# Expert feed-forward in steps of 512 columns, with gate and up panels apart and one running order across experts

## The reference

```
def swiglu(h, wg, wu, wd):
    return (jax.nn.silu(h @ wg) * (h @ wu)) @ wd

def moe_swiglu(h, router, wg, wu, wd):
    ...
    out = jnp.zeros(h.shape, jnp.float32)
    for e in range(N_EXPERTS):
        out = out + combine[..., e:e + 1] * swiglu(h, wg[e], wu[e], wd[e]).astype(jnp.float32)
```

## Time and profile before

| what | value |
|---|---|
| median of three runs | 1997.97 us |
| span of the profiled execution | 1991.5 us |
| PE busy | 1860.5 us (93%) |
| DVE busy | 1538.0 us (77%) |
| ACT busy | 1140.7 us (57%) |
| DMA moved | 485.36 MB, mean 244 GB/s |
| experts, first up matmul to last down matmul | 946.7 to 1972.4 us of the span |

### The profile page before, as it was taken

One profiled execution on the slowest core, in us unless ns is written; L12 is line 12 of the kernel. 1 busy time (PEld: TensorE's weight loads), 2 busy tenths in 40 slices (PEclk: granted clock), 3 DMA queues, 4 the chain that ended last, 5 costly groups with the idle time before them and its releaser, 6 DMA issues.

```text
span 1991.5 us, 29581 instructions
## 1 busy us (share of the span) xinstructions
PE 1860.5 (93%) x10776; PEld 1626.4 (82%) x10776; DVE 1538.0 (77%) x1598; ACT 1140.7 (57%) x1037; POOL 5.1 (0%) x13
## 2 busy tenths in 40 slices
PE   6999889899989999896999999999999999999997
PEld 6988788799979888785787887878878788788785
DVE  3979867544449799576788888879878888898886
ACT  4335544444343355543676776767767667676774
POOL 0000000000000000000000000000000000000000
PEclk9999999999988899897999999999999999999998
DMA  6434333755334344335899999999989999999993
GB/s 227 149 119 157 127 107 114 264 190 188 108 120 136 110 149 137 106 128 180 275 367 315 367 365 313 367 308 360 367 299 367 330 337 365 312 367 359 309 366 117
DMA packets 346936, 485.36 MB, mean 244 GB/s; under 512 B 16992, under 2 KB 270944, under 8 KB 346736
## 3 DMA queue, kind: packets, MB, share of 16 engines
q1 hardware_dynamic: 345808, 479.65, 71.5%
q0 software_dynamic: 1056, 4.70, 0.6%
HBM read 483.24 MB, written 1.05 MB: 243 GB/s over the span
## 4 chain that ended last, share of the span: by engine, by line
PE 75%; DVE 14%; ACT 5%; issue 4%; DMA 1%; SPq 0%; ACTq 0%; DVEq 0%
PE pair L750 53%; PE aux L750 16%; DVE lo_ring L1234 5%; ACT hi_ring L387 2%; PE aux L1134 2%; PE pair L1157 1%; DVE arena L1466 1%; DMA raw_ring<-in_w_in 1%; DVE arena L1415 1%; DVE arena L1401 1%; DVE x L1777 1%; DVE small L1414 1%; DVE pair L1391 0%; DVE arena L1480 0%; ACT arena L432 0%
## 5 line engine op out<-in xcount | busy, mean ns | idle before, releaser
L1234 DVE TENSOR_TENSOR lo_ring<-raw_ring,hi_ring 128x2048 fp32r<-128x2048 f32 (+2 forms) x278 | 623.6, 2247 | 140.3 <-ACT hi_ring L387 136.3
L387 ACT ACTIVATE hi_ring<-raw_ring 128x2048 fp32r<-128x2048 f32 (+2 forms) x278 | 521.1, 1878 | 191.3 <-PE pair L750 151.3
L1234 DVE TENSOR_TENSOR lo_ring<-arena,hi_ring 128x2048 fp32r<-128x2048 f32 x183 | 419.4, 2292 | 78.9 <-ACT hi_ring L387 72.3
L750 PE MATMUL pair<-lo_ring,hT_hi 128*128 128x512 f32 (+3 forms) x992 | 392.3, 395 | 19.9 <-DVE lo_ring L1234 17.5
L750 PE MATMUL pair<-hT_lo,hi_ring 128*128 128x256 f32 x1328 | 389.5, 293 | 20.1 <-ACT arena L432 7.7
L750 PE MATMUL pair<-hT_hi,lo_ring 128*128 128x256 f32 x1328 | 383.9, 289 | 0.0
L750 PE MATMUL pair<-hT_hi,hi_ring 128*128 128x256 f32 x1328 | 383.3, 289 | 0.0
L750 PE MATMUL pair<-hi_ring,hT_hi 128*128 128x512 f32 (+3 forms) x992 | 382.3, 385 | 0.0
L750 PE MATMUL pair<-hi_ring,hT_lo 128*128 128x512 f32 (+3 forms) x992 | 381.3, 384 | 0.0
L387 ACT ACTIVATE hi_ring<-arena 128x2048 fp32r<-128x2048 f32 x183 | 349.4, 1914 | 46.2 <-PE pair L750 36.2
L750 PEld LDWEIGHTS pair<-hT_lo,hi_ring 128*128 128x128 f32 x1328 | 263.1, 198 | 27.9 <-ACT arena L432 10.0
(11 more groups left out here) (277 smaller groups left out, 1984.8 us busy)
## 6 DMA issues: line engine op xcount, KB each, us to landing
arena<-in_md SPq DMA_DIRECT2D x128, 512.0 KB, 5.7
raw_ring<-in_w_in SPq DMA_DIRECT2D x120, 512.0 KB, 4.5
raw_ring<-in_mg SPq DMA_DIRECT2D x120, 512.0 KB, 5.4
raw_ring<-in_mu SPq DMA_DIRECT2D x120, 512.0 KB, 6.4
arena<-in_mg SPq DMA_DIRECT2D x104, 512.0 KB, 5.2
arena<-in_mu SPq DMA_DIRECT2D x104, 512.0 KB, 6.2
raw_ring<-in_md SPq DMA_DIRECT2D x96, 512.0 KB, 5.2
raw_ring<-in_w_br SPq DMA_DIRECT2D x32, 512.0 KB, 4.6
```

Of the source, the lines that this page charges most:

```text
L387: nc.scalar.activation(hi_ring[:, h, 0:cols], raw(slot)[:, 0:cols], ACT.Copy).then_inc(hi_ready, 1)
L750: ins = pe.matmul(out, l, r, start=first and n == 0, stop=last and n == 2, skip_group_check=True)
L1234: nc.vector.tensor_tensor(lo_ring[:, h, 0:cols], raw(slot)[:, 0:cols], hi_ring[:, h, 0:cols].bitcast(f32), ALU.subtract).then_inc(lo_ready, 1)
```

## The change

An expert now has seven steps of 512 hidden columns with six panels each: two gate panels, two up panels, and the two down panels of the step before it. Gate goes into the first bank of `pair0` and up into its second, transposes go into `pair1`; there is no alternation. The order gate, up, down of the step before runs on through the end of an expert: the two last down panels of an expert stand in the first step of the next. The gather of the next expert's tokens is moved to step 5, ahead of its down panels, `hx_hi` and `hx_lo` to the end of step 6. `turn_pick` is in step 3, the scatters in step 1, one ahead of the down panels and one behind them. Each engine has one loop per expert with all seven steps written out. Rows of gate and up weights that a DMA reads are 512 columns (2 KB) instead of 256 (1 KB). Since the last down panels no longer end inside the loop, they follow it after the branch that skips the extra blocks.

```diff
--- before.py
+++ after.py
-EXP_STEPS = F_EXP // STEP_F
+EXP_F = 512
+EXP_STEPS = F_EXP // EXP_F
...
-EXP_PANELS = 3 * EXP_STEPS
+EXP_PANELS = 6 * EXP_STEPS
...
-        hid_hi = sb("hid_hi", [128, 2, STEP_F], f32r)
-        hid_lo = sb("hid_lo", [128, 2, STEP_F], f32r)
+        hid_hi = sb("hid_hi", [128, EXP_F], f32r)
+        hid_lo = sb("hid_lo", [128, EXP_F], f32r)
...
+        def exp_at(n, k):
+            return k if isinstance(n, int) and n == 0 else 6 * n - 2 + k
+        def exp_slot(n, k):
+            return k if isinstance(n, int) and n == 0 else (4 + k) % FRING
+        def exp_use(n, k):
+            return 0 if isinstance(n, int) and n == 0 else (n - 1 if k < 2 else n)
...
+            def exp_panel(n, k, src, width):
+                slot = exp_slot(n, k)
+                p = EXP_BASE + exp_at(n, k)
+                v = raw(slot).rearrange("p (k n) -> p k n", n=width)
+                h = v.shape[1] // 2
+                sp.wait_ge(lo_ready, p - (FRING - 1))
+                sp.dma_start(v[:, 0:h, :], src[:, 0:h, :]).then_inc(raw_in[slot], 16)
+                sp.dma_start(v[:, h:2 * h, :], src[:, h:2 * h, :]).then_inc(raw_in[slot], 16)
+            def exp_up(n, e, s):
+                for w, k0 in ((mg, 0), (mu, 2)):
+                    for kh in range(2):
+                        exp_panel(n, k0 + kh, w[bass.ds(e, 1), kh * 512:(kh + 1) * 512, s * EXP_F:(s + 1) * EXP_F]
+                                  .rearrange("a (k p) n -> p (a k) n", p=128), EXP_F)
+            def exp_down(n, e, s):
+                for q in range(2):
+                    r = s * EXP_F + q * 256
+                    exp_panel(n, 4 + q, md[bass.ds(e, 1), r:r + 256, :].rearrange("a (k p) n -> p (a k) n", p=128), D)
+            def expert(j, e, before):
+                n0 = j * EXP_STEPS
+                for s in range(EXP_STEPS):
+                    exp_up(n0 + s, e, s)
+                    if s:
+                        exp_down(n0 + s, e, s - 1)
+                    elif before is not None:
+                        exp_down(n0, before, EXP_STEPS - 1)
+            expert(0, 0, None)
+            with sp.Fori(1, NE) as j:
+                expert(j, j, j - 1)
...
+            def exp_silu(n):
+                act.wait_ge(panel_used, EXP_BASE + exp_at(n, 1) + 1)
+                act.wait_ge(S["hid_done"], DENSE_STEPS + n)
+                nc.scalar.activation(ar(A_SG, EXP_F), pairs[0][:, 0:EXP_F], ACT.Silu).then_inc(S["gu_silu"], 1)
+            def exp_hid_hi(n):
+                act.wait_ge(S["hid_turned"], n + 1)
+                nc.scalar.activation(hid_hi[:, :], pairs[1][:, 0:EXP_F], ACT.Copy).then_inc(S["hid_hi_done"], 1)
...
+                for s in range(EXP_STEPS):
+                    n = j * EXP_STEPS + s
+                    if not (first and s == 0):
+                        exp_hi(n, 0)
+                        exp_hi(n, 1)
+                    exp_hi(n, 2)
+                    if not (first and s == 0):
+                        exp_hid_hi(n - 1)
+                    if s == 1 and not first:
+                        output_hi(j - 1, EXP_BASE + exp_at(j * EXP_STEPS, 5) + 1)
+                    exp_hi(n, 3)
+                    if not (first and s == 0):
+                        exp_hi(n, 4)
+                    exp_silu(n)
+                    if not (first and s == 0):
+                        exp_hi(n, 5)
+                    if s == 3:
+                        pickT_copy(j)
+                act.wait_ge(panel_used, EXP_BASE + exp_at((j + 1) * EXP_STEPS - 1, 3) + 1)
+                hx_hi(j + 1)
...
+            exp_end = (m + NE) * EXP_STEPS
+            for q in range(2):
+                to_hi(EXP_BASE + exp_at(exp_end, q), exp_slot(1, q), EXP_USE0[exp_slot(1, q)] + exp_use(exp_end, q), PANEL,
+                      (EXP_BASE + exp_at(1, q)) % HRING)
+                if q == 0:
+                    exp_hid_hi(exp_end - 1)
+            output_hi(m + (NE - 1), EXP_BASE + exp_at(exp_end, 1) + 1)
...
+            def exp_weights(n, k, width):
+                h = (EXP_BASE + (k if isinstance(n, int) and n == 0 else exp_at(1, k))) % HRING
+                pe.wait_ge(lo_ready, EXP_BASE + exp_at(n, k) + 1)
+                return weights(h, width)
+            def exp_up(n):
+                for g in range(2):
+                    for kh in range(2):
+                        w = exp_weights(n, 2 * g + kh, EXP_F)
+                        for k in range(4):
+                            a = (4 * kh + k) * 128
+                            ins = split_mm(pairs[0][:, g * EXP_F:(g + 1) * EXP_F], (hxh[:, a:a + 128], hxl[:, a:a + 128]),
+                                           (w[0][:, k, :], w[1][:, k, :]), kh == 0 and k == 0, kh == 1 and k == 3)
+                        ins.then_inc(panel_used, 1)
+            def exp_turn(n):
+                pe.wait_ge(S["hid_done"], DENSE_STEPS + n + 1)
+                for k in range(EXP_F // 128):
+                    ins = pe.transpose(pairs[1][:, k * 128:(k + 1) * 128], ar(A_HID + k * 128, 128), C("ident"))
+                ins.then_inc(S["hid_turned"], 1)
+            def exp_down(n, k0, s):
+                pe.wait_ge(S["hid_lo_done"], DENSE_STEPS + n)
+                for q in range(2):
+                    w = exp_weights(n, k0 + q, 512)
                     for half in range(2):
                         for k in range(2):
-                            ins = split_mm(aux[:, half * 512:(half + 1) * 512],
-                                           (hid_hi[:, s0 % 2, k * 128:(k + 1) * 128], hid_lo[:, s0 % 2, k * 128:(k + 1) * 128]),
+                            o = (2 * q + k) * 128
+                            ins = split_mm(aux[:, half * 512:(half + 1) * 512], (hid_hi[:, o:o + 128], hid_lo[:, o:o + 128]),
                                            (w[0][:, 2 * k + half, :], w[1][:, 2 * k + half, :]),
-                                           s0 == 0 and k == 0, s0 == EXP_STEPS - 1 and k == 1)
+                                           s == 0 and q == 0 and k == 0, s == EXP_STEPS - 1 and q == 1 and k == 1)
                     ins.then_inc(panel_used, 1)
 
+            def turn_pick(j, first):
+                if not first:
+                    pe.wait_ge(S["x_added"], 2 * j)
+                for b in range(NB):
+                    ins = pe.matmul(aux[:, 1024 + b * 128:1152 + b * 128], pick[:, b, :], ident_r[:, :], start=True, stop=True)
+                ins.then_inc(S["pick_turned"], 1)
+            def expert(j, first=False):
                 pe.wait_ge(S["hx_lo_done"], j + 1)
...
+                for s in range(EXP_STEPS):
+                    n = j * EXP_STEPS + s
+                    exp_up(n)
+                    if s == 1 and not first:
+                        scatter(j - 1, 0)
+                    if s == 3:
+                        turn_pick(j, first)
+                    if s == 5:
+                        pe.wait_ge(S["pickT_done"], j + 1)
+                        gather(j + 1)
+                    if s:
+                        exp_down(n, 4, s - 1)
+                    elif not first:
+                        exp_down(n, 4, EXP_STEPS - 1)
+                    if s == 1 and not first:
+                        scatter(j - 1, 1)
+                    exp_turn(n)
...
+            exp_down((m + NE) * EXP_STEPS, 0, EXP_STEPS - 1)
...
+            def exp_hid(n):
+                dve.wait_ge(S["gu_silu"], DENSE_STEPS + n + 1)
+                dve.wait_ge(panel_used, EXP_BASE + exp_at(n, 3) + 1)
+                if not (isinstance(n, int) and n == 0):
+                    dve.wait_ge(S["hid_turned"], n)
+                nc.vector.tensor_tensor(ar(A_HID, EXP_F), pairs[0][:, EXP_F:2 * EXP_F], ar(A_SG, EXP_F), ALU.mult)\
+                  .then_inc(S["hid_done"], 1)
+            def exp_hid_lo(n):
+                dve.wait_ge(S["hid_hi_done"], DENSE_STEPS + n + 1)
+                nc.vector.tensor_tensor(hid_lo[:, :], pairs[1][:, 0:EXP_F], hid_hi[:, :].bitcast(f32), ALU.subtract)\
+                  .then_inc(S["hid_lo_done"], 1)
...
+                for s in range(EXP_STEPS):
+                    n = j * EXP_STEPS + s
+                    opening = first and s == 0
+                    if not opening:
+                        exp_lo(n, 0)
+                        exp_lo(n, 1)
+                    exp_lo(n, 2)
+                    if not opening:
+                        exp_hid_lo(n - 1)
+                    if s == 1 and not first:
+                        output_lo(j - 1)
+                    if s == 4:
+                        dve.wait_ge(S["pickT_done"], j + 1)
+                        make_pick(j + 1)
+                    exp_lo(n, 3)
+                    if not opening:
+                        exp_lo(n, 4)
+                        exp_lo(n, 5)
+                    exp_hid(n)
+                    if s == 1 and not first:
+                        add(j - 1, 0)
+                    if s == 2 and not first:
+                        add(j - 1, 1)
```

(28 more changed lines are left out.)

108 lines of the change are left out of this document (26 added, 82 removed).

## The result

The changed kernel takes 1970.14 us, the median of six runs (1960.30 to 1971.33), beside 1996.64 for six runs of the kernel before (1988.46 to 2001.74). These medians lie 26.5 us apart; the ratio on record isn't that of the medians, it is 0.9847 with a 95% interval of 0.9826 to 0.9867, which is 30.5 us less (26.6 to 34.7). Forecast were 1966 us in a range of 1957 to 1985, and faster. Both held.

The account below looks back on a forecast made before the run. PE's matmul stream was taken to bound the experts, with the rest to be won where an expert ends. Terms summed to -32.2 us: span 1991.5 to 1959.3, plus 6.5 outside, about 1966 us, range 1957 to 1985.

Parts of the forecast that it names:

- (a): Between experts: PE's wait for the next expert's tokens goes, 2.59 us seven times, 18.1 us less.
- (b): Behind the token wait: slow clock after idle PE goes, 1.57 us at four of seven boundaries, 6.3 us less.
- (c): `turn_pick` and the turn behind it: no wait for DVE's late product, 0.81 x 7 = 5.7 us less.
- (d): First scatter and the turn behind it: scatters now lie between panels without waits, 0.32 x 7 = 2.2 us less.
- (e): Turns inside experts: one of four transposes replaces two of two, 56 steps of 512 save 3.1 us.
- three tight places: Handover, output split in step 1, second add in step 2: 0.2, 0.2, 0 us spare; cost 0, range 0 to 1 each.
- (f): First expert: the product stands ahead of the next gate panel's lo on DVE, 0.9 us lost.
- (g): End of last expert: 1.6 us wait for the last split plus 0.7 for a hi part, 2.3 us lost.
- Tight places: Rival: tokens 1 us later, other tight places 0.3 each, slow clock at four of seven boundaries; 1983 us, chance 0.14.
- DVE as the bound: Rival: longer lo parts or a late product let DVE set the step; 2033 us at 2.8 per part, chance 0.07.
- Loop code that doesn't stay: Rival: PE's longer loop body is fetched anew at six returns, up to 29.7 us; 1995.6 or about 1981, chance 0.10.
- The 6.5 us outside it: Program time beyond the profiled span: 1997.97 - 1991.5, added to the span of 1959.3 to give 1965.8 us.

Follow-up runs that it names:

- late_tokens: Changed kernel with gather, `hx_hi` and `hx_lo` put back behind the turn of an expert's last step; 1988.59 us, ratio 0.9950.
- filled kernel: Kernel before the change, with 18 matmuls of unused result ahead of PE's wait for the tokens at seven boundaries; 1990.22 us, ratio 0.9954.
- one loop: Changed kernel with the number of extra blocks read before the first expert and a single loop over all blocks; 1962.93 us, ratio 0.9823.

## Why the prediction was right, and where it was not

**(a) The wait for the tokens, 18.1.** Right. No wait of PE at the handover is left; late_tokens brought 7 x 2.5 back.

**(b) The slow clock behind it, 6.3.** Right: 6.8 in the filled kernel, and 1.00 at the handovers after. The late tokens cost 1.9 each for it instead of 0.9 per handover, as all seven fell and not four, three of them for 6.8 us and not 3.4. So this term belongs to an execution of a given kernel, not to the code alone.

**(c), (d), (e) `turn_pick`, scatter and turns, 5.7 + 2.2 + 3.1.** Right in sum. The time of one expert can be read from PE's branch at the end of the loop (line, duration min/median/max in ns, first and last start), which answers to the earlier trace rows:

```profile
L1284 PEldq COMPARE_BRANCH  x7: 83/215/217, 1185.1 to 1925.9; - x7
L1288 PEldq COMPARE_BRANCH  x1: 3591/3591/3591, 1926.9 to 1926.9; - x1
```

(1925.9 - 1185.1) / 6 = 123.47 us, forecast 123.4. Before it was 127.57 without slow clock; less 2.59 for the wait, 1.51 per expert is left for these three terms, 1.55 forecast. (The 1.51 is net of the 0.2 that is lost in step 2, see the tight places.) The two places themselves:

```profile
1099.15 0.39 PE L1272 MATMUL aux<-hT_lo,pickT 128*128 128x512 f32 x1
...
1100.06 0.60 PE L1221 MATMUL pair<-consts,arena 128*128 128x128 f32 x4
1100.42 0.47 PE L815 MATMUL pair<-lo_ring,hT_hi 128*128 128x512 f32 x1
...
1128.43 0.33 PE L1241 MATMUL aux<-ident_r,pick 128*128 128x128 f32 x2
1128.60 0.45 PE L815 MATMUL aux<-lo_ring,hid_hi 128*128 128x512 f32 x1
```

The turn follows the scatter's four matmuls after 0.91, without a wait, and `turn_pick` costs 0.17; with its turn it took 1.17 in the earlier trace rows. A turn of four costs 0.36 until the next panel starts and, from the step of 16.78 less 6 x 2.72, 0.46 in all; I had taken 0.49.

**The three tight places, taken at 0.** Right for two; the third costs 0.2 us per expert. The handover, on ACT (`hx_hi`, then two hi parts) and on DVE (product, `hx_lo`, two lo parts), start and duration:

```profile
1182.94 1.03 ACT L733 ACTIVATE hT_hi<-aux 128x1024 fp32r<-128x1024 f32 x1 [0.88 <-PE pair L815]
1183.86 3.71 ACT L432 ACTIVATE hi_ring<-arena 128x2048 fp32r<-128x2048 f32 x2
```
```profile
1184.30 0.68 DVE L1826 TENSOR_TENSOR arena<-pair,arena 128x512 f32<-128x512 f32 x1
1184.90 1.22 DVE L1813 TENSOR_TENSOR hT_lo<-aux,hT_hi 128x1024 fp32r<-128x1024 f32 x1
1186.03 4.48 DVE L1308 TENSOR_TENSOR lo_ring<-arena,hi_ring 128x2048 fp32r<-128x2048 f32 x2
```

The lo parts start at 1186.03, and 2.35 later, by the handover of the prediction, is 1188.38; PE starts at 1188.46. So 0.1 us is to spare where I had 0.2. The forecast was right by little, and it isn't shown how much more DVE may take at this place before PE waits.

In step 1, with the split of the finished output, no gap of PE shows. Behind step 2, with the second add to x on DVE, one does:

```profile
1116.85 0.60 PE L1221 MATMUL pair<-consts,arena 128*128 128x128 f32 x4
1117.41 0.50 PE L815 MATMUL pair<-lo_ring,hT_hi 128*128 128x512 f32 x1
...
1117.41 0.19 PEld L815 LDWEIGHTS pair<-lo_ring,hT_hi 128*128 128x128 f32 x1 [0.20 <-DVE lo_ring L1308]
```

The panel follows the turn after 0.56 instead of 0.36, and the step takes 17.00 instead of 16.79, in each of the seven experts of the loop. That is 0.2 x 7 = 1.5 us, where the prediction took 0 and left 0 to 1 each for the range. It is this wait that the waits view shows seven times.

**(f) The first expert, +0.9.** Right: from first up matmul to the next step's are 16.99, forecast 16.86. The rows answer to the earlier trace rows.

```profile
943.40 0.79 PE L815 MATMUL pair<-lo_ring,hT_hi 128*128 128x512 f32 x1 [2.37 <-DVE hT_lo L1813]
...
960.39 0.50 PE L815 MATMUL pair<-lo_ring,hT_hi 128*128 128x512 f32 x1 [1.54 <-DVE lo_ring L1308]
```

**(g) The end, +2.3: the step that failed.** The term measured 6.9 us, the 2.3 forecast and 4.6 more. The prediction wrote of the branch out of the loop, "PE's queue runs some 3 us ahead of its matmuls [...], so most of it falls into the same wait; up to 3.4 more [...] stays in the range." PE, from the last turn on:

```profile
1928.86 0.60 PE L1221 MATMUL pair<-consts,arena 128*128 128x128 f32 x4
...
1930.95 0.49 PE L815 MATMUL aux<-lo_ring,hid_hi 128*128 128x512 f32 x1 [1.49 <-DVE hid_lo L1831]
1933.66 0.79 PE L815 MATMUL aux<-hi_ring,hid_lo 128*128 128x512 f32 x1 [2.21 <-issue]
1934.25 0.63 PE L815 MATMUL aux<-hi_ring,hid_hi 128*128 128x512 f32 x1
...
1941.38 0.39 PE L815 MATMUL aux<-hi_ring,hid_hi 128*128 128x512 f32 x1
```

The branch itself did what I said: begun at 1926.9, it was over at 1930.5, and the first down matmul came at 1930.95, 2.09 behind the turn, which is the forecast 0.49 + 1.6 with nothing of the branch in it. But behind this one matmul PE stops for 2.71 us with 2.21 of "issue", and then runs at the slow clock: 0.74 over 13 us, 6.8 us at the 1.2 GHz level. The two panels take 10.43 from first to last start, against 5.97 with one loop: 4.5 us more than I had, the 4.6 that the experts' stretch is short of the forecast.

What makes the gap is shown in part. The rows of one kernel with the same branch, late_tokens, have it at 3432 ns and no gap behind it: 5.97 from first to last down matmul. The kernel with 1 KB rows has 3404 ns and a gap of 2.28. So the branch as such doesn't cost PE time. Between 1925 and 1950 us the DMA queue q8, which brings instructions in packets of 16 KB, has three packets in the changed kernel and three in that with 1 KB rows, but none with one loop. (A second instruction queue, with packets of 8 KB, has three, three and one.) In the changed kernel q8's packets start at 1927.9, 1931.2 and 1934.9. The second lies beside the gap; the third comes when PE is running again. This is q8 over 1931 to 1934 us:

```profile
q8 instruction: 1, 0.02, 2.4%
```

late_tokens has two such packets, at 1948.6 and 1951.8, and no third. Its second one starts 0.14 us after the first down matmul, much as in the changed kernel (0.27), and yet PE doesn't stop. This fits code behind the branch that isn't there yet, with the place of the code deciding how many matmuls get through before the next block is needed. But it is an argument: what is shown is that the gap goes with the branch over the unused loop (one loop) and that the branch doesn't always bring it (late_tokens). The cause of the gap itself stays open.

**The rivals.** Tight places: false at the handover, by 0.1 us, where the rival wanted 1 us and the slow clock; one of the other two places cost 0.2. DVE as the bound: false in these runs, since its lo part took 2.29 as before (the page has 2289 ns as the mean of 183) and PE waits for it in no step but for the 0.2 us named above; how far it is from the point where it would decide wasn't tried. Loop code that doesn't stay: false. Over 1200 to 1900 us nothing but weights moved, as the queues show (packets, MB, share of 16 engines):

```profile
DMA packets 109507, 250.59 MB, mean 358 GB/s; under 512 B 7645, under 2 KB 7645, under 8 KB 109507
...
q1 hardware_dynamic: 109507, 250.59, 98.3%
```

and PE's returns took 0.215 with a body of 609 rows. q8 has five packets of 16 KB in the loop's first pass (at 1075.5 to 1181.5 us) and no other before 1927.9. The Trainium skill ("Runtime: NRT & Kernel Launch", instruction fetch mechanics) gives PE 128 KiB for instructions; by that rule this body stays, and the trace agrees. By its remark of only two lines of 16 KiB the body would be fetched anew in each round, and the trace contradicts it.

**The sum.** Terms (a) to (f) together were good to a microsecond and (g) was 4.6 too small. The stretches outside the experts came out 4.7 shorter, so the span agrees, 1959.1 for 1959.3: two errors that cancel by luck. The 6.5 us outside it where 1.8 belong moved the forecast up by 4.7, by luck again towards a median that lies 9 us above the profiled execution. That execution is one of the two at 1960, with a clock of 0.967; I put the 9 us down to the first stretch, where the clock varies, but no execution at 1970 was profiled. What speaks for it: the profile of the kernel with 1 KB rows is 5.4 us longer, its first stretch 5.7 longer, and its experts the same.

## What to carry to other kernels

Where the busiest engine is full inside a loop's body, look at what the body's end hands to its start: here a wait of 2.6 us per round, with the clock that it cost, was some 25 us of 2000 (18.1 + 6.8), and 31 when it was put back into the changed kernel. Inputs made early, together with a running order that keeps independent panels between a result and its use, removed it whole; neither did so alone. Fill or split a wait if it can't be removed; two waits of 1 us cost the waits alone, one of 2.4 cost the clock as well in eleven of fourteen places. For a span, compare only stretches whose code the change touches, and take what lies outside the span from the same execution.

## What was not expected of the hardware

- An idle time of PE of 2.4 to 2.5 us at the handover came with a slow clock of 3.4 us in four of seven places in the kernel before and of 3.4 or 6.8 us in seven of seven in late_tokens; idle times of 1.0 and 0.8 us within 4 us came with none, in seven places.
- A taken branch over code that had not run took 3.38 to 3.59 us on PE's queue in the six kernels that have it, and was hidden behind queued matmuls. A further stop of 2.2 to 2.3 us came one matmul behind it in the changed kernel and that with 1 KB rows, and not in late_tokens.
- Rows of 2 KB and 4 KB together arrived at 358 GB/s over 700 us. Between 1 KB and 2 KB rows for gate and up PE's time didn't differ (0.3 us of 998), though 1 KB rows had been seen at 348 and 4 KB rows at 397 GB/s.
